# Two-layer hybrid attention and SwiGLU trunk on one core: the fifth pair of the down projection joins the two-step Strassen scheme, and the top steps move forward

## The chip, the cores and the metric

The kernel runs on one core of a Trainium2 chip. A core has five engines with queues of their own: TensorE (PE, matmuls), VectorE (DVE), ScalarE (ACT), GpSimd (POOL) and SyncE (SP, here the queue of the DMAs). The metric is the device time of one execution in microseconds (us); a lower one is better.

## What is computed

Two layers over a sequence of 256 tokens of width 1024, all in fp32. The part that the change touches is the last statement of each layer, the SwiGLU block and its down projection (`D_FF` is 2816):

```python
def hybrid_layer(x, ...):
    h = rms_norm(x, g_attn_pre)
    proj = einsum(h, w_in) + b_in
    ...                                  # MoBA and sliding-window attention
    x = x + rms_norm(einsum(mix, w_out), g_attn_post)
    h = rms_norm(x, g_ffn_pre)
    f = silu(h @ w_gate) * (h @ w_up)
    x = x + rms_norm(f @ w_down, g_ffn_post)
```

## The kernel before

**Tiling.** The tokens are two tiles `t` of 128. Weights come from HBM in blocks of 128 x 2048 numbers (1 MB) in the order of the list `BLOCKS`, each into one of three places of `raw`. ScalarE writes a rounded copy of a block (`hi`, L698) into one of four slots `w_h`, VectorE writes what the rounding left (`lo`, L985) into `w_l`, and TensorE multiplies block b as high x high, high x low and low x high, three matmuls for each product. A block of four k-tiles and 512 columns, or of two k-tiles and 1024 columns, costs 24 matmuls for both token tiles. `hi` of block b waits until TensorE is through with block b - 4 (`after(L, b)` handles block b + 4), and a load waits for the `lo` of the block that had its place.

**The SwiGLU part.** `FF` is cut into six chunks `c` of 512 columns (the last has 256). A chunk from 1 to 4 has four blocks, gate twice and up twice; chunk 5 has two. When both are multiplied, VectorE forms f (`swiglu`, L1189) and transposes it in blocks of 32 (`squares_f`, L1200), and GpSimd carries the 32-blocks across partitions with 16 copies (`exchange`, L638). ScalarE and VectorE then split the result into high and low parts in chunk c + 1 (`hi_f`, `lo_f` L1207).

**The down projection** is f (two token tiles, 22 k-tiles) times `w_down` (two halves of 512 columns). For k-tile pairs 0 to 4 the 2 x 2 x 2 block product is done by Strassen's scheme in Winograd's form with seven products in place of eight. Four of them (M1, M6, M5, M7) are summed over the pairs in banks 4 to 7 and are joined once at the end (`join`, L1258); three go straight into the result banks. The sums of f that the scheme needs, s1 to s4, are made by VectorE for the pairs of chunks 0, 1 and 2 (`add_s` L1217 to L1220, then `hi_s` on ScalarE L745 and `lo_s` on VectorE L1225). The sums of the weights are made in `raw` by `add_top` (L1235 to L1239, five instructions of 512 columns), which waits for the block's load.

- Pairs 0 to 3 go in two steps. The **top** step (`top(L, n)`, 12 matmuls, L1514) does the four shared products. It stands behind the last block of chunk n + 2, and waits for the low part of its block, of f, and of the sums s of chunk n // 2 (`summed`). The **bottom** step (`bottom(L, n)`, 9 matmuls) does the other three, between the down blocks, with half a block loaded again and the kept sum T4.
- Pair 4 goes in one piece, `squares`, behind the last bottom step: its block is loaded raw, VectorE makes all sums (`add_squares`, L1248 to L1252), and there are two splits of it, "raw" (1536 columns) and "sum" (2048 columns, `lo` at L976), for 9 and 12 matmuls.

The rest of the k-tiles (10 to 21) are plain down blocks: two among the bottom steps, four behind them ("late" ones, from `FIRST_LATE` on). The first late block is multiplied by token tile 0 only after `join_first` has added to its banks.

**What sets the order.** Each engine's program is written out by hand and runs strictly in order; they meet by counting semaphores. In chunk 1 VectorE's program ends with swiglu, the two transposes, `lo` of the next block, and then `lo_s(L, 0)`; the first `add_top` opens its part of chunk 2.

## Time and profile before

| | us |
|---|---|
| median of 3 runs | 562.53 |
| lowest, highest | 562.33, 562.94 |
| the profiled execution | 562.32 |
| its span | 560.5 |
| TensorE busy | 552.5 |
| VectorE busy | 454.7 |
| ScalarE busy | 308.7 |
| GpSimd busy | 248.9 |

The profiled execution's time is 1.8 us above its span, and 0.2 us under the median. The busy time of TensorE counts a matmul until its modelled end, which overlaps the next one's start: what one matmul costs is the distance between two starts in the timeline, and a short pause shows there as a longer distance, often without being listed as a wait.

### The profile page before, as it was taken

What the parts mean: (1) busy time and instruction counts of PE and PEld (TensorE: products, weight loads), DVE (VectorE), ACT (ScalarE), POOL (GpSimd) and SP (SyncE); (2) the same over time, 40 slices, a digit from 0 to 9 for tenths busy, and PEclk for the clock granted to TensorE, in tenths of its full rate; (3) what the DMA queues carried; (4) which work ended last, traced back from release to release, by engine and by line L of the source; (5) the groups of instructions that cost most, each with busy time, mean ns of one, the idle gap of its engine ahead of it and who ended that gap; (6) DMA issues with size and microseconds to landing.
All of it is one profiled execution on the core that took longest, in us unless ns stands there. A gap on an engine that the chain in (4) does not pass through costs nothing.

```text
span 560.5 us, 8816 instructions
## 1 busy us (share of the span) xinstructions
PE 552.5 (99%) x3346; PEld 454.1 (81%) x3346; DVE 454.7 (81%) x592; ACT 308.7 (55%) x438; POOL 248.9 (44%) x307
## 2 busy tenths in 40 slices
PE   8999999999999999999999999999999999999996
PEld 6878888888888888887888888888888888888774
DVE  6799996856879788789898998675848889878993
ACT  6576775555444633566547658574643635436540
POOL 1101132406396786954220055232076696965910
PEclk9999999999999999999999999999999999999999
DMA  8964533648445654477566344425573546536821
GB/s 347 373 227 145 202 105 161 229 160 313 163 177 220 232 195 187 146 255 269 227 248 214 134 170 151 187 88 215 229 258 151 224 151 230 209 124 197 291 76 75
DMA packets 19195, 111.55 MB, mean 199 GB/s; under 512 B 2384, under 2 KB 2768, under 8 KB 7632
## 3 DMA queue, kind: packets, MB, share of 16 engines
q1 hardware_dynamic: 19152, 110.97, 53.7%
q8 instruction: 27, 0.44, 0.3%
q14 instruction: 16, 0.13, 0.1%
HBM read 109.92 MB, written 1.05 MB: 198 GB/s over the span
## 4 chain that ended last, share of the span: by engine, by line
PE 47%; POOL 22%; DVE 16%; issue 5%; ACT 5%; DMA 4%; DVEq 0%; SPq 0%; POOLq 0%; ACTq 0%
PE bank L1499 39%; POOL work L638 20%; DVE w_l L985 4%; DMA raw<-in_w_blocks 3%; PE bank L1612 3%; DVE work L1200 2%; POOL mixed_crossed L622 2%; ACT w_h L698 2%; PE bank L1597 2%; PE bank L1638 1%; DMA work<-in_first_rest 1%; PE bank L1514 1%; DVE work L1189 1%; DVE fT_l L1207 1%; PE bank L1665 1%
## 5 line engine op out<-in xcount | busy, mean ns | idle before, releaser
L985 DVE TENSOR_TENSOR w_l<-raw,w_h 128x2048 fp32r<-128x2048 f32 x90 | 206.6, 2307 | 58.4 <-ACT w_h L698 58.0
L638 POOL COPY work<-work 32x256 f32<-32x256 f32 (+1 forms) x192 | 188.6, 982 | 107.4 <-DVE work L1200 79.8
L698 ACT ACTIVATE w_h<-raw 128x2048 fp32r<-128x2048 f32 x90 | 169.7, 1904 | 109.1 <-DVE raw L1239 65.5
L1499 PE MATMUL bank<-w_h,actT_h 128*128 128x512 f32 (+1 forms) x568 | 223.6, 394 | 0.2
L1499 PE MATMUL bank<-w_h,actT_l 128*128 128x512 f32 (+1 forms) x568 | 219.9, 387 | 0.0
L1499 PE MATMUL bank<-w_l,actT_h 128*128 128x512 f32 (+1 forms) x568 | 218.0, 386 | 0.0
L1499 PEld LDWEIGHTS bank<-w_h,actT_h 128*128 128x128 f32 x568 | 106.8, 188 | 23.1 <-issue 2.0
L1499 PEld LDWEIGHTS bank<-w_h,actT_l 128*128 128x128 f32 x568 | 106.7, 188 | 22.0
L1499 PEld LDWEIGHTS bank<-w_l,actT_h 128*128 128x128 f32 x568 | 106.8, 188 | 20.3
L612 POOL TENSOR_TENSOR norms<-norms,constants 128x1 f32<-128x1 f32 x8 | 4.8, 601 | 93.8 <-ACT bank L814 93.6
L787 ACT ACTIVATE work<-bank,neg_max 128x128 f32<-128x128 f32 (+1 forms) x64 | 25.9, 425 | 9.9 <-DVE neg_max L1102 9.9
L1612 PE MATMUL bank<-ident,work 128*128 128x128 f32 x216 | 29.6, 273 | 0.0
L1612 PEld LDWEIGHTS bank<-ident,work 128*128 128x128 f32 x216 | 25.4, 140 | 4.3
L1514 PE MATMUL bank<-w_h,fT_h 128*128 128x512 f32 x70 | 27.5, 393 | 0.3 <-DVE w_l L976 0.2
L1514 PE MATMUL bank<-w_l,fT_h 128*128 128x512 f32 x70 | 27.3, 390 | 0.0
L1514 PE MATMUL bank<-w_h,fT_l 128*128 128x512 f32 x70 | 27.2, 389 | 0.0
L587 POOL TENSOR_TENSOR norms<-norms,constants 128x1 f32<-128x1 f32 x8 | 10.8, 1354 | 36.9 <-ACT work L755 36.9
L622 POOL COPY mixed_crossed<-mixed_squares 32x128 f32<-32x128 f32 x48 | 19.2, 399 | 13.7 <-DVE mixed_squares L1139 11.8
L764 ACT ACTIVATE work<-bank 128x512 f32<-128x512 f32 x16 | 9.6, 599 | 28.4 <-PE bank L1499 28.4
L595 POOL TENSOR_TENSOR norms<-norms,constants 128x1 f32<-128x1 f32 x8 | 6.6, 822 | 40.2 <-ACT work L764 40.2
L1154 DVE TENSOR_TENSOR work<-bank,gain_b 128x512 f32<-128x512 f32 x16 | 10.7, 687 | 12.6 <-ACT work L764 12.6
L1499 PE MATMUL bank<-w_h,fX_h 128*128 128x512 f32 x64 | 20.6, 393 | 0.2
(123 smaller groups left out, 635.2 us busy)
## 6 DMA issues: line engine op xcount, KB each, us to landing
raw<-in_w_blocks SPq DMA_DIRECT2D x90, 1024.0 KB, 4.8
raw<-in_w_blocks SPq DMA_DIRECT2D x8, 512.0 KB, 4.2
gains<-in_b_in SPq DMA_DIRECT2D x8, 256.0 KB, 5.7
work<-in_first_rest SPq DMA_DIRECT2D x3, 512.0 KB, 6.1
raw<-in_second_block SPq DMA_DIRECT2D x2, 512.0 KB, 8.1
x<-in_x SPq DMA_DIRECT2D x2, 512.0 KB, 13.8
gain_b<-in_g_attn_post SPq DMA_DIRECT2D x2, 512.0 KB, 8.1
gains<-in_g_ffn_pre SPq DMA_DIRECT2D x2, 512.0 KB, 6.9
```

The source lines that it names most:

```text
L587: nc.gpsimd.tensor_tensor(ss_x[:, t:t + 1], ss_x[:, t:t + 1], eps, ALU.add).then_inc(eps_added, 1)
L622: ins = nc.gpsimd.tensor_copy(mixed_crossed[t][32 * j:32 * j + 32, i * P:(i + 1) * P], mixed_squares[t][32 * i:32 * i + 32, j * P:(j + 1) ...
L638: ins = nc.gpsimd.tensor_copy(work[32 * j:32 * j + 32, 4:6, i * n:(i + 1) * n], work[32 * i:32 * i + 32, 6:8, j * n:(j + 1) * n])
L698: nc.scalar.activation(w["h"][:, slot(L, b), at:], raw[:, r, at:], ACT.Copy).then_inc(hi_ready, 1)
L787: last = nc.scalar.activation(probs[g, r][:, j, n * keys:(n + 1) * keys], bank[b][:, n * keys:(n + 1) * keys], ACT.Exp, bias=neg_max[:, g, ...
L985: nc.vector.tensor_tensor(w["l"][:, slot(L, b), at:], raw[:, raw_slot(L, b), at:], w["h"][:, slot(L, b), at:].bitcast(F32), ALU.subtract). ...
L1154: nc.vector.tensor_tensor(y[t][:, c, :], bank[b][:], gain_b[:, c * BANK:(c + 1) * BANK], ALU.mult).then_inc(drained[b], 1)
L1200: nc.vector.transpose(squares[t][:, 0:n].rearrange("p (j k b) -> p j k b", j=4, b=32), f[t][:, 0:n].rearrange("p (k j b) -> p j k b", j=4, ...
L1499: ins = nc.tensor.matmul(bank[BANK_OF[name]][:, 0:n], left[s][:, k, :], right[r][:, k, c * BANK:c * BANK + n], start=first and k == 0 and ...
L1514: ins = nc.tensor.matmul(out_[:], left[s], right[r], start=first and (s, r) == ("h", "h"), stop=last and (s, r) == ("l", "h"))
L1597: ins = nc.tensor.matmul(bank[BANK_OF[name]][:, 0:n], actT[s][:, k, tokens(t)], right[r][:, k, :], start=first, stop=last and (s, r) == pr ...
L1612: ins = nc.tensor.transpose(out_[:, q * P:(q + 1) * P], src(q), ident[:])
```

## The change

- **Pair 4 goes in two steps** like the others: `TOPS` is 5, `squares`, `add_squares`, the blocks "raw" and "sum" and their splits are gone. There is a fifth top block, `top(L, 4)` behind the last block of chunk 5, a fifth bottom block, and a tile `t4_last` for its T4. The matmuls are the same in number: 12 + 9 for the pair in either form.
- **The top steps move forward.** `top(L, n)` for n from 0 to 3 stands behind the first block of chunk n + 2, ahead of the chunk's other blocks. In VectorE's program `add_top(L, n)` moves from the chunk of its use into the chunk ahead of it, `add_top(L, 0)` into chunk 1.
- **Loads.** The half blocks of bottom steps 0 and 1 come in one load of 1 MB, as do those of 2 and 3; the fifth is loaded alone.
- **Joining.** M1 is copied out (`keep_m1`) already behind the last top step, and the two sums that only need the top products are made earlier (`sum_products`).

The diff, its core:

```diff
 CHUNK_AT = []
-TOPS = 4
+TOPS = 5
 TOP_AT = []
 for c in range(FFN_CHUNKS):
     CHUNK_AT += [len(BLOCKS)]
     if c < FF // BANK:
-        BLOCKS += [(m, k, 4, c * BANK, BANK) for m in ("gate", "up") for k in (0, 4)]
+        parts = [(m, k, 4, c * BANK, BANK) for m in ("gate", "up") for k in (0, 4)]
     else:
-        BLOCKS += [("both", k, 4, c * BANK, BANK) for k in (0, 4)]
+        parts = [("both", k, 4, c * BANK, BANK) for k in (0, 4)]
+    BLOCKS += parts[:1]
     if c >= 2:
         TOP_AT += [len(BLOCKS)]
         BLOCKS += [("top", 2 * (c - 2), 2, 0, D)]
+    BLOCKS += parts[1:]
 LAST = FFN_CHUNKS - 1
-LAST_COLS = FF - LAST * BANK
+TOP_AT += [len(BLOCKS)]
+BLOCKS += [("top", 2 * TOPS - 2, 2, 0, D)]
+
+
+def part_at(c, q):
+    return CHUNK_AT[c] + q + (1 if c >= 2 and q else 0)
+
+
 FIRST_DOWN = len(BLOCKS)
 KF = FF // P
 
 
 
 
...
         BLOCKS += [("bot", 2 * len(BOT_AT) - 2, 2, 0, D)]
-RAW_AT = len(BLOCKS)
-BLOCKS += [("raw", 2 * TOPS, 2, 0, D), ("sum", 2 * TOPS, 2, 0, D)]
+BOT_AT += [len(BLOCKS)]
+BLOCKS += [("bot", 2 * TOPS - 2, 2, 0, D)]
 FIRST_LATE = len(BLOCKS)
 BLOCKS += [("down", k, 2, 0, D) for k in (14, 16, 18, 20)]
 NB = len(BLOCKS)
-LOADED = [b for b in range(NB) if BLOCKS[b][0] != "sum"]
+
+LOADED = [b for b in range(NB) if b not in BOT_AT[1::2]]
 NL = len(LOADED)
 STORED = [b for b in LOADED if BLOCKS[b][0] != "bot"]
...
+    return L * NL + LOADED.index(b - 1 if b in BOT_AT[1::2] else b)
 
 
 def raw_slot(L, b):
@@ -118,6 +127,11 @@
     return (load_count(L, b) // RAW + 1) * 16
 
 
+def bot_cols(b):
+    at = BOT_AT.index(b) % 2
+    return slice(2 * BANK * at, 2 * BANK * (at + 1))
+
+
 def freed_by(b):
...
                     past_L, past = divmod(load_count(L, b) - RAW, NL)
-                    place_free(lo_ready, past_L * NB + LOADED[past] + 1)
-                    if BLOCKS[LOADED[past]][0] == "raw":
-                        place_free(sums_ready, past_L + 1)
+                    place_free(lo_ready, past_L * NB + LOADED[past] + (2 if LOADED[past] in BOT_AT[:-1] else 1))
                 if BLOCKS[b][0] == "bot":
-                    top = STORED.index(TOP_AT[BOT_AT.index(b)])
-                    sp.dma_start(raw[:, r, 0:2 * BANK], w_blocks[L, top, :, 2 * BANK:4 * BANK]).then_inc(raw_in[r], 16)
+                    n = BOT_AT.index(b)
+                    at = [STORED.index(top) for top in TOP_AT[n:n + 2]]
+                    tops = slice(at[0], at[-1] + 1, at[-1] - at[0] or 1)
+                    sp.dma_start(raw[:, r, 0:2 * BANK * len(at)].rearrange("p (a n) -> p a n", a=len(at)),
+                                 w_blocks[L, tops, :, 2 * BANK:4 * BANK].rearrange("a p n -> p a n")
+                                 ).then_inc(raw_in[r], 16)
                 else:
...
 
-                act.wait_ge(block_used, USED.done(L, FIRST_LATE - 2) + USED.n)
+                act.wait_ge(block_used, USED.done(L, TOP_AT[-1]) + USED.n)
                 nc.scalar.activation(m1_sum, products[0][:], ACT.Copy).then_inc(m1_kept, 1)
...
                 for c in range(1, FFN_CHUNKS):
-                    b = CHUNK_AT[c]
-                    after(L, b)
+                    after(L, part_at(c, 0))
+                    if c >= 2:
+                        after(L, TOP_AT[c - 2])
                     silus(L, c, 0)
                     silus(L, c, 1)
-                    after(L, b + 1)
+                    after(L, part_at(c, 1))
                     if c < FFN_CHUNKS - 1:
-                        after(L, b + 2)
+                        after(L, part_at(c, 2))
                         hi_f(L, c - 1, 0)
                         hi_f(L, c - 1, 1)
                         if c <= FAST_CHUNKS:
                             hi_s(L, c - 1)
-                        after(L, b + 3)
-                    if c >= 2:
-                        after(L, TOP_AT[c - 2])
+                        after(L, part_at(c, 3))
+                    else:
+                        after(L, TOP_AT[TOPS - 1])
                 hi_f(L, FFN_CHUNKS - 2, 0)
                 hi_f(L, FFN_CHUNKS - 2, 1)
-                for b in range(FIRST_DOWN, RAW_AT):
+                after(L, FIRST_DOWN)
...
+                keep_m1(L)
+                for b in range(FIRST_DOWN + 1, FIRST_LATE - 2):
                     after(L, b)
-                keep_m1(L)
                 hi_f(L, FFN_CHUNKS - 1, 0)
                 hi_f(L, FFN_CHUNKS - 1, 1)
-                after(L, RAW_AT)
-                after(L, RAW_AT + 1)
+                after(L, FIRST_LATE - 2)
+                after(L, FIRST_LATE - 1)
                 sum_y(L, 1, 0)
                 if L < depth - 1:
...
                 x = bank[BANK_OF["down", t, c]]
                 nc.vector.tensor_tensor(x[:], x[:], what, ALU.add).then_inc(joined, 1)
 
-            def join_first(L):
+            def sum_products(L):
 
                 _, m6, m5, _ = products
                 dve.wait_ge(m1_kept, L + 1)
+                link(L, nc.vector.tensor_tensor(u2, m1_sum, m6[:], ALU.add))
+                link(L, nc.vector.tensor_tensor(u4, u2, m5[:], ALU.subtract))
+
+            def join_first(L):
+
+                dve.wait_ge(products_full, L + 1)
                 join(L, 0, 0, m1_sum)
-                dve.wait_ge(products_full, 3 * L + 1)
-                link(L, nc.vector.tensor_tensor(u2, m1_sum, m6[:], ALU.add))
-                dve.wait_ge(products_full, 3 * L + 2)
-                link(L, nc.vector.tensor_tensor(u4, u2, m5[:], ALU.subtract))
                 join(L, 0, 1, u4)
 
             def join_second(L):
 
                 _, _, m5, m7 = products
-                dve.wait_ge(products_full, 3 * L + 3)
                 link(L, nc.vector.tensor_tensor(u3, u2, m7[:], ALU.add))
                 dve.wait_ge(second_begun, L + 1)
                 join(L, 1, 0, u3)
...
                 for c in range(1, FFN_CHUNKS):
-                    b = CHUNK_AT[c]
-                    end = b + (1 if c == FFN_CHUNKS - 1 else 3)
-                    if 2 <= c < FFN_CHUNKS - 1:
-                        add_top(L, c - 2)
-                    if c == FFN_CHUNKS - 1:
-                        swiglu(L, c, 0)
-                    for q in range(b, end):
-                        after(L, q)
+                    after(L, part_at(c, 0))
+                    if c >= 2:
+                        after(L, TOP_AT[c - 2])
                     if c < FFN_CHUNKS - 1:
+                        add_top(L, c - 1)
+                        after(L, part_at(c, 1))
+                        after(L, part_at(c, 2))
                         if c <= FAST_CHUNKS:
                             add_s(L, c - 1)
                         lo_f(L, c - 1, 0)
@@ -1398,30 +1389,29 @@
                         squares_f(L, c, 1)
                         if c == FFN_CHUNKS - 2:
                             add_top(L, TOPS - 1)
-                        after(L, end)
+                        after(L, part_at(c, 3))
                         if c <= FAST_CHUNKS:
                             lo_s(L, c - 1)
                     else:
+                        swiglu(L, c, 0)
+                        after(L, part_at(c, 1))
                         swiglu(L, c, 1)
-                        after(L, end)
-                    if c >= 2:
-                        after(L, TOP_AT[c - 2])
+                        after(L, TOP_AT[TOPS - 1])
                 for t in range(T):
                     lo_f(L, FFN_CHUNKS - 2, t)
                 for t in range(T):
                     squares_f(L, FFN_CHUNKS - 1, t)
                 after(L, FIRST_DOWN)
                 after(L, BOT_AT[0])
-                add_squares(L)
+                sum_products(L)
                 after(L, BOT_AT[1])
                 after(L, BOT_AT[1] + 1)
                 after(L, BOT_AT[2])
                 join_first(L)
                 after(L, BOT_AT[3])
-                after(L, RAW_AT)
                 lo_f(L, FFN_CHUNKS - 1, 0)
                 lo_f(L, FFN_CHUNKS - 1, 1)
-                after(L, RAW_AT + 1)
+                after(L, BOT_AT[4])
                 join_second(L)
                 scale_y(L, 1, 0)
                 update_x(L, 1, 0)
...
                 pe.wait_ge(lo_ready, L * NB + b + 1)
-                product(m1, a11, b11, n == 0, False)
-                product(m6, s2, t2, n == 0, False)
-                product(m5, s1, t1, n == 0, False)
-                product(m7, s3, t3, n == 0, False).then_inc(block_used, 1)
+                last = n == TOPS - 1
+                product(m1, a11, b11, n == 0, last)
+                product(m6, s2, t2, n == 0, last)
+                product(m5, s1, t1, n == 0, last)
+                product(m7, s3, t3, n == 0, last).then_inc(block_used, 1)
                 USED.tick(b)
 
             def bottom(L, n):
...
-                product(x12, s4, b22, False, False)
-                product(x11, a12, b21, False, False)
-                product(x21, a22, t4, False, False).then_inc(block_used, 1)
+                last = n == TOPS - 1
+                product(x12, s4, b22, False, last)
+                ins = product(x11, a12, b21, False, last)
+                if last:
+                    ins.then_inc(products_full, 1)
+                product(x21, a22, t4, False, last).then_inc(block_used, 1)
                 USED.tick(b)
-
-            def squares(L):
-
...
                 multiply(L, 1, b + 2)
                 multiply(L, 1, b + 3)
                 for c in range(1, FFN_CHUNKS):
-                    b = CHUNK_AT[c]
                     for q in range(2 if c == FFN_CHUNKS - 1 else 4):
-                        multiply(L, 0, b + q)
-                        multiply(L, 1, b + q)
-                    if c >= 2:
-                        top(L, c - 2)
+                        multiply(L, 0, part_at(c, q))
+                        multiply(L, 1, part_at(c, q))
+                        if c >= 2 and q == 0:
+                            top(L, c - 2)
+                top(L, TOPS - 1)
...
```

**VectorE, chunk 1 of layer 0, before.** The rows are, in turn, swiglu twice, the two transposes, `lo` of a block, `lo_s(0)` (L1225), and then the first `add_top` (five rows).

```order
L1189 SCALAR_TENSOR_TENSOR work<-bank3,norms,work 128x512 [waits squares_ready0,drained2,full3]
L1189 SCALAR_TENSOR_TENSOR work<-bank1,norms,work 128x512 [waits squares_ready1,drained0,full1]
L1200 STREAM_TRANSPOSE work<-work 128x512 [waits crossed_in,drained3]
L1200 STREAM_TRANSPOSE work<-work 128x512 [waits crossed_in,drained1]
L985 TENSOR_TENSOR w_l<-raw,w_h 128x2048 [waits hi_ready]
L1225 TENSOR_TENSOR fT_l<-work,fT_h 128x1024 [waits s_hi_ready]
L1235 TENSOR_TENSOR raw<-raw 128x512 [waits raw_in1]
L1236 TENSOR_TENSOR raw<-raw 128x512
L1237 TENSOR_TENSOR gains<-raw 128x512
L1238 TENSOR_TENSOR gains<-gains,raw 128x512 [waits dve_step]
L1239 TENSOR_TENSOR raw<-raw 128x512
```

**VectorE, the same place now** (its lines are numbered 6 higher in the changed file): `add_top(0)` is the rows L1241 to L1245, then `lo` of two blocks, then `add_s(0)`.

```order
L1241 TENSOR_TENSOR raw<-raw 128x512 [waits raw_in1]
L1242 TENSOR_TENSOR raw<-raw 128x512
L1243 TENSOR_TENSOR gains<-raw 128x512
L1244 TENSOR_TENSOR gains<-gains,raw 128x512 [waits dve_step]
L1245 TENSOR_TENSOR raw<-raw 128x512
L991 TENSOR_TENSOR w_l<-raw,w_h 128x2048 [waits hi_ready] x2
L1223 TENSOR_TENSOR work<-work 128x256 [waits crossed_in]
L1224 TENSOR_TENSOR work<-work 128x256
L1225 TENSOR_TENSOR work<-work 128x256 [waits dve_step]
```

The rest of the chunk, down to `lo_s(0)` (L1231):

```order
L1195 SCALAR_TENSOR_TENSOR work<-bank3,norms,work 128x512 [waits squares_ready0,drained2,full3]
L1195 SCALAR_TENSOR_TENSOR work<-bank1,norms,work 128x512 [waits squares_ready1,drained0,full1]
L1206 STREAM_TRANSPOSE work<-work 128x512 [waits crossed_in,drained3]
L1206 STREAM_TRANSPOSE work<-work 128x512 [waits crossed_in,drained1]
L991 TENSOR_TENSOR w_l<-raw,w_h 128x2048 [waits hi_ready]
L1231 TENSOR_TENSOR fT_l<-work,fT_h 128x1024 [waits s_hi_ready]
L991 TENSOR_TENSOR w_l<-raw,w_h 128x2048 [waits hi_ready] x2
```

`lo_s(0)` keeps its place behind both swiglu and a `lo`, and the five additions have gone ahead of two `lo`.

**TensorE, chunk 2 of layer 0, behind its first block, before.** The next block follows.

```order
L1499 MATMUL bank0<-w_h,actT_h 128x512
L1499 MATMUL bank0<-w_l,actT_h 128x512
L1499 MATMUL bank0<-w_h,actT_l 128x512
L1499 MATMUL bank2<-w_h,actT_h 128x512 [waits lo_ready]
L1499 MATMUL bank2<-w_l,actT_h 128x512
L1499 MATMUL bank2<-w_h,actT_l 128x512
L1499 MATMUL bank2<-w_h,actT_h 128x512
```

**TensorE, the same place now.** L1504 with banks 4 to 7 is the top step.

```order
L1489 MATMUL bank0<-w_h,actT_h 128x512
L1489 MATMUL bank0<-w_l,actT_h 128x512
L1489 MATMUL bank0<-w_h,actT_l 128x512
L1504 MATMUL bank4<-w_h,fT_h 128x512 [waits lo_ready,s_lo_ready,f_lo_ready]
L1504 MATMUL bank4<-w_l,fT_h 128x512
L1504 MATMUL bank4<-w_h,fT_l 128x512
L1504 MATMUL bank5<-w_h,fT_h 128x512
```

The first top step now stands where the second block of chunk 2 stood; before, it came 72 matmuls (three blocks) later.

**VectorE, the end of layer 0, before:** `add_squares`, `lo` of "raw", of "sum" and of the first late block, `join_first`, two more `lo`.

```order
L981 TENSOR_TENSOR w_l<-gains,w_h 128x512
L979 TENSOR_TENSOR w_l<-raw,w_h 128x1024 [waits hi_ready]
L981 TENSOR_TENSOR w_l<-gains,w_h 128x512
L1248 TENSOR_TENSOR work<-raw 128x1024 [waits raw_in0]
L1251 TENSOR_TENSOR work<-work,raw 128x512 [waits dve_step]
L1252 TENSOR_TENSOR work<-raw,work 128x512 [waits dve_step]
L985 TENSOR_TENSOR w_l<-raw,w_h 128x1536 [waits hi_ready]
L976 TENSOR_TENSOR w_l<-work,w_h 128x2048 [waits hi_ready]
L985 TENSOR_TENSOR w_l<-raw,w_h 128x2048 [waits hi_ready]
L1258 TENSOR_TENSOR bank2<-bank2,work 128x512 [waits m1_kept]
L1266 TENSOR_TENSOR work<-work,bank5 128x512 [waits products_full]
```

**VectorE, the same place now:** `sum_products`, `lo` of the fifth bottom block, of two late blocks, `join_first`.

```order
L988 TENSOR_TENSOR w_l<-gains,w_h 128x512
L986 TENSOR_TENSOR w_l<-raw,w_h 128x1024 [waits hi_ready]
L988 TENSOR_TENSOR w_l<-gains,w_h 128x512
L1256 TENSOR_TENSOR work<-work,bank5 128x512 [waits m1_kept]
L1257 TENSOR_TENSOR work<-work,bank6 128x512 [waits dve_step]
L986 TENSOR_TENSOR w_l<-raw,w_h 128x1024 [waits hi_ready,dve_step]
L988 TENSOR_TENSOR w_l<-t4_last,w_h 128x512
L991 TENSOR_TENSOR w_l<-raw,w_h 128x2048 [waits hi_ready] x2
```

Three additions and two splits are gone; `join_first` has two instructions in place of four, and stands behind two late blocks in place of one.

## Rows read from the trace of the kernel before

**Rows 1.** the page, busy time of each engine: us, share of the span, instructions.
```profile
PE 552.5 (99%) x3346; PEld 454.1 (81%) x3346; DVE 454.7 (81%) x592; ACT 308.7 (55%) x438; POOL 248.9 (44%) x307
```

**Rows 2.** timeline of TensorE (start us, us, what), first matmuls of three top steps.
```profile
168.37 0.39 PE L1514 MATMUL bank<-w_h,fT_h 128*128 128x512 f32 x1
...
230.93 0.39 PE L1514 MATMUL bank<-w_h,fT_h 128*128 128x512 f32 x1
...
443.07 0.39 PE L1514 MATMUL bank<-w_h,fT_h 128*128 128x512 f32 x1
```

**Rows 3.** timeline of TensorE, end of layer 0.
```profile
254.50 0.39 PE L1514 MATMUL bank<-w_h,fT_l 128*128 128x512 f32 x1
254.95 0.50 PE L1514 MATMUL bank<-w_h,fT_h 128*128 128x512 f32 x1
...
257.85 0.39 PE L1499 MATMUL bank<-w_h,fX_h 128*128 128x512 f32 x1
...
261.70 0.39 PE L1499 MATMUL bank<-w_h,fX_l 128*128 128x512 f32 x1
...
262.71 0.62 PE L1499 MATMUL bank<-w_l,fX_h 128*128 128x512 f32 x2
```

**Rows 4.** timeline of TensorE, end of layer 1.
```profile
529.22 0.39 PE L1514 MATMUL bank<-w_h,fT_l 128*128 128x512 f32 x1
...
532.66 0.62 PE L1499 MATMUL bank<-w_h,fX_h 128*128 128x512 f32 x2
...
536.51 0.39 PE L1499 MATMUL bank<-w_h,fX_l 128*128 128x512 f32 x1
...
537.57 0.62 PE L1499 MATMUL bank<-w_l,fX_h 128*128 128x512 f32 x2
```

**Rows 5.** timeline of VectorE, end of layer 0.
```profile
227.95 4.69 DVE L985 TENSOR_TENSOR w_l<-raw,w_h 128x2048 fp32r<-128x2048 f32 x2 [1.99 <-ACT w_h L698]
...
252.50 2.40 DVE L976 TENSOR_TENSOR w_l<-work,w_h 128x2048 fp32r<-128x2048 f32 x1 [0.23 <-ACT w_h L690]
254.82 2.37 DVE L985 TENSOR_TENSOR w_l<-raw,w_h 128x2048 fp32r<-128x2048 f32 x1
...
259.75 4.48 DVE L985 TENSOR_TENSOR w_l<-raw,w_h 128x2048 fp32r<-128x2048 f32 x2
```

**Rows 6.** timeline of VectorE, chunk 1 of layer 0 and the step behind it.
```profile
132.50 2.48 DVE L985 TENSOR_TENSOR w_l<-raw,w_h 128x2048 fp32r<-128x2048 f32 x1 [1.49 <-ACT w_h L698]
...
143.38 2.29 DVE L985 TENSOR_TENSOR w_l<-raw,w_h 128x2048 fp32r<-128x2048 f32 x1 [2.52 <-ACT w_h L698]
...
148.11 1.40 DVE L1189 SCALAR_TENSOR_TENSOR work<-bank,norms,work 128x512 f32<-128x512 f32 x2
...
152.82 1.42 DVE L1225 TENSOR_TENSOR fT_l<-work,fT_h 128x1024 fp32r<-128x1024 f32 x1
154.16 0.88 DVE L1235 TENSOR_TENSOR raw<-raw 128x512 f32<-128x512 f32 x1
```

**Rows 7.** timeline of VectorE, layer 1.
```profile
427.52 1.42 DVE L1225 TENSOR_TENSOR fT_l<-work,fT_h 128x1024 fp32r<-128x1024 f32 x1
```

**Rows 8.** timeline of ScalarE, chunks 1 and 2 of layer 0.
```profile
141.43 1.92 ACT L698 ACTIVATE w_h<-raw 128x2048 fp32r<-128x2048 f32 x1 [3.01 <-PE bank L1499]
...
158.28 1.92 ACT L698 ACTIVATE w_h<-raw 128x2048 fp32r<-128x2048 f32 x1 [8.12 <-DVE raw L1239]
```

**Rows 9.** timeline of GpSimd, the exchange of chunk 0 (16 copies).
```profile
131.14 10.86 POOL L638 COPY work<-work 32x256 f32<-32x256 f32 x16 [20.02 <-DVE work L1200]
```

**Rows 10.** groups by line, GpSimd, from 131.1, 138.5 and 150.8 us on.
```profile
L638 POOL COPY work<-work 32x256 f32<-32x256 f32 x3 | 1.2, 393 | 20.1 <-DVE work L1200 20.0
...
L638 POOL COPY work<-work 32x256 f32<-32x256 f32 x2 | 2.8, 1379 | 0.1
...
L638 POOL COPY work<-work 32x256 f32<-32x256 f32 x7 | 7.4, 1059 | 9.1 <-DVE work L1200 8.8
```

**Rows 11.** a stretch behind the last matmul; the clock stands behind POOL.
```profile
555.00:559.00 4.00, 0.00 (x0) 0.00 (x0) 2.24 (x5) 0.69 (x2) 0.55 (x1) 0.93 0.20 73
```

More of the change, by code:

```diff
@@ L130, in completes @@
     m, k0, nk, col, n = BLOCKS[b]
-    if m in ("down", "raw", "sum", "top", "bot"):
+    if m in ("down", "top", "bot"):
         return [("down", t, c) for c in range(2)] if k0 + nk == KF else []
@@ L256, in trunk @@
         fT = {s: sb("fT_" + s, [P, 39, P], F32R) for s in "hl"}
-        sums = work_row[:, 0:4 * BANK].rearrange("p (a n) -> p a n", a=2)
-        t4_kept = [gains[:, n * BANK:(n + 1) * BANK] for n in range(TOPS)]
+        t4_kept = [gains[:, n * BANK:(n + 1) * BANK] for n in range(4)] + [sb("t4_last", [P, BANK])[:]]
         m1_sum = rope_tmp
@@ L672, in hi @@
                 m, k0 = BLOCKS[b][0:2]
-                if m == "sum":
-                    act.wait_ge(sums_ready, L + 1)
-                elif m == "top":
+                if m == "top":
                     r = raw_slot(L, b)
@@ L688, in hi @@
                     act.wait_ge(block_used, USED.done(L, last % NB) + (USED.n if last >= 0 else 0))
[L689 to L693 removed]
+                if m == "bot":
+                    nc.scalar.activation(w["h"][:, slot(L, b), 0:2 * BANK], raw[:, r, bot_cols(b)], ACT.Copy)
                     nc.scalar.activation(w["h"][:, slot(L, b), 2 * BANK:3 * BANK], t4_kept[BOT_AT.index(b)], ACT.Copy
@@ L973, in lo @@
                 m, k0 = BLOCKS[b][0:2]
-                if m == "sum":
-                    low, high = (w[s][:, slot(L, b), :].rearrange("p (a n) -> p a n", a=2) for s in "lh")
-                    nc.vector.tensor_tensor(low, sums, high.bitcast(F32), ALU.subtract).then_inc(lo_ready, 1)
-                elif m == "bot":
+                if m == "bot":
                     high, low = (w[s][:, slot(L, b), :] for s in "hl")
-                    nc.vector.tensor_tensor(low[:, 0:2 * BANK], raw[:, raw_slot(L, b), 0:2 * BANK],
+                    nc.vector.tensor_tensor(low[:, 0:2 * BANK], raw[:, raw_slot(L, b), bot_cols(b)],
                                             high[:, 0:2 * BANK].bitcast(F32), ALU.subtract)
@@ L1880 @@
     arrays["w_blocks"] = np.empty((depth, len(STORED), P, BLOCK), np.float32)
-    weights["raw"] = weights["down"].reshape(depth, FF, 2, BANK)[:, :, ::-1].reshape(depth, FF, D)
-    weights["top"] = weights["raw"]
+    weights["top"] = weights["down"].reshape(depth, FF, 2, BANK)[:, :, ::-1].reshape(depth, FF, D)
     for b, at in enumerate(STORED):
```

51 lines of the change are left out of this document (5 added, 46 removed).

## The prediction

> **What bounds the kernel now.** I read the page's busy times first: TensorE works 552.5 of 560.5 us [rows 1]. VectorE has a fifth of its time free, but runs in order, so its place in its program matters, not its sum. The change takes no matmul away (12 + 9 for pair 4 in either form), so the time can only move by TensorE's pauses. The list of waits hardly shows them; I looked for them in the timeline, as starts further apart than the pitch. The pitch: from the first matmul of the first top step to that of the fourth, at 168.37 and 230.93 [rows 2], lie three top steps and ten blocks, 3 x 12 + 10 x 24 = 276 matmuls, so 62.56 / 276 = 0.2267 us each.
>
> Between 254.50 and 257.85 [rows 3] stand 13 matmuls: 3.35 us where 2.95 would do, a pause of 0.40. It is the "sum" half of pair 4: its low part (L976) ends at 252.50 + 2.40 = 254.90 [rows 5], and the next matmul starts at 254.95. Of the 0.40, 0.22 are the wait and 0.18 the slow start behind it. Between 261.70 and 262.71 stand three matmuls (a row with "x2" between them): 1.01 for 0.68, a pause of 0.33; it waits for the `lo` of the second late block, which begins at 259.75 and takes 2.24 [rows 5]. Layer 1 has the same two, 3.44 - 2.95 = 0.49 and 1.06 - 0.68 = 0.38 [rows 4]. In all 1.60 us: that is everything the end of the layers can give back.
>
> **The change part by part.**
>
> *The first top step moves forward.* It was reached at 168.37 and comes three blocks, 72 x 0.2267 = 16.32 us, earlier: TensorE reaches it at 152.05. It waits for `lo_s(0)`, the low part of the sums s of chunk 0. VectorE does that at the end of its part of chunk 1: it starts at 152.82 and takes 1.42, so it is done at 154.24 [rows 6]. Before, that was 14 us of cover; now it is 2.2 us too late. With the lag of 0.05 seen at 254.90 / 254.95, TensorE starts again at 154.29: 2.24 us of waiting, and 0.15 for the slow start (0.18 above, here between that and 0.1). Nothing can run meanwhile, since TensorE's program is in order. Layer 1: 443.07 - 16.32 = 426.75 [rows 2] against 427.52 + 1.42 + 0.05 = 428.99 [rows 7], again 2.24. Cost: 2 x 2.39 = 4.8 us. The other three moved steps need the sums of chunks 0 and 1, made a chunk or more before, and wait for none.
>
> *`add_top(0)` in chunk 1 of VectorE.* Its five additions take from 154.16 [rows 6] until ScalarE starts at 158.28 [rows 8]: 4.1 us. They now stand behind the `lo` that ends at 134.98, and end at about 139.0; the block's `hi` takes 1.92, so its `lo` runs from 141.0 to 143.2. The next `lo`, at 143.38, waits for a `hi` of 141.43 that TensorE releases, and is not moved. VectorE idled here; its cover is 0.2 us, and everything behind 143.38, `lo_s(0)` too, stays where it was. So this costs nothing, if the exchange of chunk 0 is not held up. That one took 10.86 us from 131.14 to 142.0 [rows 9]; `add_s` needs it at 145.6 (the `lo` of 143.38 and 2.2). A copy takes 0.39 us beside an idle VectorE, 1.38 beside a `lo`, and 1.06 in a stretch with one `lo`, the `lo_s` and five additions, seven copies for seven instructions [rows 10]. I count 3 copies up to 132.5, 2 beside the `lo`, 5 beside the additions, 5 in the idle 2.0 us behind them, and the last beside the next `lo`: it ends by 143.2. I take 0. With 1.38 beside the additions too (3 copies), and 0.6 in the idle time, the last copy ends at 146.0 to 146.4: up to 0.8 us per layer, the upper end.
> The Trainium skill (SBUF — State Buffer, "Who interferes with whom") says that a VectorE instruction with two SBUF inputs and a GpSimd one that reads SBUF fully block each other for an instruction's length; by that rule copies pass between instructions and the five short additions let five through, which is the 0; by a rate in proportion to busy time it would be the 0.8 above. The seven for seven agree with the rule, the two beside one `lo` don't quite.
>
> *The other moved and added steps.* From chunk 2 on VectorE has as many steps per chunk as before. `add_top(4)` stands where `add_top(3)` stood. The low part of that block was done at 227.95 + 2.35 = 230.3 [rows 5], for a step reached at 230.93; top 4 is reached 12 matmuls later, a cover of 3.3 us. The pause above gives the helpers 2.2 us more on top. No cost, and if that cover were gone, TensorE would wait for the rest, one to one.
>
> *The end of the layer.* VectorE loses three additions and two splits (L976 alone 2.40) and gains one split of 1536 columns. The low part of the fifth bottom block comes before that of the first late block, long before use, so both old pauses go: -1.60 us. One new meeting is close. The first late block's `hi` waits for the down block ahead of bottom steps 2, 3, 4. Call that block's end T. ScalarE starts 0.26 behind such an end (141.43 against 152.05 - 48 x 0.2267 = 141.17), VectorE 1.95 later (143.38), two `lo` follow at 2.24 to 2.37 each [rows 5], then the join, a quarter of what `join_first` took, (259.75 - 257.19) / 4 = 0.64: T + 7.3 to 7.6. TensorE is there after 3 x 9 + 6 = 33 matmuls, T + 7.48. Between nothing and 0.25 with its slow start, I take 0.05 per layer: +0.1.
>
> *Loads.* One load of 1 MB more and four half ones turned into two whole and a half: SP's queue holds fewer, and no pause of TensorE stands behind a load. Price 0; a pair load comes from two places, whose speed no row shows, but it is asked for 8 us and more before its `hi`, against 5 for a load.
>
> **Sum:** 4.78 + 0.10 - 1.60 = +3.3 us. The profiled execution took 562.32, so 565.6; the median is 0.2 above it, so **565.7**.
>
> **The rivals.**
>
> *The exchange is held up.* Then `lo_s(0)` is 0.4 to 0.8 later in both layers, or the close meeting at the join costs 0.25 too: 565.7 + 1.6 = 567.3, at most 567.9. For it: GpSimd's copies are slow beside `lo`. Against: one copy per short instruction.
>
> *The clock falls in the pause.* In the 4 us from 555.0 on, with no matmul, the mean clock is 0.93 [rows 11]: full for 3.44 us, then the lower level, 1.2 for 2.4 GHz. The pause here is 2.2 us, with matmuls before and behind. If it fell all the same, matmuls would start 0.45 apart for a time; at 4 us of that per layer, 2 us each: 569.7.
> The Trainium skill (TensorE: Matmul & The Clock Gate, "HAM oscillation — how this bites in real kernels") tells of kernels whose clock falls in each wait between bursts of matmuls; that rule is this rival.
>
> *Not slower.* `lo_s(0)` would have to be done much earlier. VectorE has swiglu, transposes, a `lo` and `lo_s` behind the last matmul of chunk 1; these run from 148.11 to 154.24, 6.1 us [rows 6], while that matmul is done at 152.05 - 5.44 + 0.2 = 146.8. If the 1.3 us of backlog before them were gone, the pause would be 0.94 and the total 2 x (0.94 + 0.15) + 0.1 - 1.60 = +0.7, 563.2. It decides from 1.3 us of pause per layer down. Against: the diff leaves that backlog as it is, and sets more work before it. A gain of 1.1 would need a pause under 0.2, less than the 6.1 us of work allow after one block of 5.44.
>
> **How the numbers follow.** The forecast has 0.72, held up 0.16, the clock 0.05, not slower 0.04, and 0.03 for something else. The forecast alone spans 564.9 (a join without wait and slow starts of 0.05) to 566.6 (one layer held up, or the join at 0.25); with the first rival 567.9. The range 564.6 to 567.9 leaves out the clock and the not-slower case. A measurement tells 0.2%, 1.1 us, from no change: slower 0.94, same 0.04, faster 0.02.
>
> **What would show it.** In the changed kernel's timeline TensorE's first matmul into bank 4 of the first top step starts 2.2 us behind its predecessor's pitch, released by VectorE's low part of the sums (L1231), at about 154.3 and 428 to 429; `add_top(0)` ends near 139.0 and the exchange by 143 to 144; the pauses before the late blocks are gone. It is wrong if that matmul starts at 152, if `lo_s(0)` ends later than 155, or if the clock falls below full.

## The result: 1.0% slower, and out of the range

| | median us | runs us | ratio, 95% interval |
|---|---|---|---|
| before, beside it | 562.74 | 562.33 to 564.50 (6) | |
| changed | 569.45 | 566.61 to 569.68 (5) | 1.0103 (1.0078 to 1.0127) |
| forecast | 565.7 | 564.6 to 567.9 | |

Slower was right, the size was not: the medians lie 6.7 us apart, and 3.3 were forecast. (The ratio in the table is not that of the medians, 1.012, which lies inside its interval. Two executions of all that follow, 1434.51 us of the changed kernel and 695.71 us of the one with 4 matmuls in the pause, were disturbed, by what is not known, and are left out.) The profiled execution took 569.68 us, with a span of 567.9, 7.4 more than that of before.

The place that the prediction spoke of is the first top step of each layer. TensorE's timeline of the changed kernel, layer 0 (start us, us, what, idle time before and who ended it):

```profile
152.10 0.39 PE L1489 MATMUL bank<-w_h,actT_l 128*128 128x512 f32 x1
155.02 0.47 PE L1504 MATMUL bank<-w_h,fT_h 128*128 128x512 f32 x1 [2.53 <-issue]
155.32 0.40 PE L1504 MATMUL bank<-w_l,fT_h 128*128 128x512 f32 x1
...
156.49 0.59 PE L1504 MATMUL bank<-w_h,fT_h 128*128 128x512 f32 x1
156.88 0.63 PE L1504 MATMUL bank<-w_l,fT_h 128*128 128x512 f32 x1
157.31 0.63 PE L1504 MATMUL bank<-w_h,fT_l 128*128 128x512 f32 x1
...
160.13 0.39 PE L1489 MATMUL bank<-w_h,actT_h 128*128 128x512 f32 x1
```

The last matmul of the block starts at 152.10, the first of `top(L, 0)` at 155.02. Less the pitch that is a pause of 2.92 - 0.23 = 2.69 us; predicted were 2.24. The profile names no releaser ("issue"); VectorE's timeline below shows what it waits for. What follows it was hardly expected: matmuls start 0.24 apart for 1.5 us, and then 0.39 to 0.43 apart up to 159.87. From 155.02 to 160.13 stand 15 matmuls, 5.11 us where 3.40 would do: 1.71 us more. The windows give the reason (length; busy time and instructions of PE, PEld, DVE, ACT, POOL; the granted clock; DMA):

```profile
153.00:154.00 1.00, 0.00 (x0) 0.00 (x0) 1.00 (x2) 1.00 (x1) 0.96 (x2) 1.00 0.00 0
155.00:156.00 1.00, 0.98 (x4) 0.85 (x5) 1.00 (x1) 0.00 (x0) 0.96 (x2) 1.00 0.81 279
156.00:157.00 1.00, 1.00 (x5) 0.79 (x4) 1.00 (x1) 0.00 (x0) 1.00 (x1) 0.75 0.95 401
157.00:158.00 1.00, 1.00 (x4) 0.80 (x3) 0.32 (x1) 0.00 (x0) 0.96 (x2) 0.50 0.71 295
...
160.00:161.00 1.00, 1.00 (x6) 0.83 (x5) 0.00 (x0) 1.00 (x1) 0.92 (x3) 1.00 0.95 401
432.00:433.00 1.00, 0.00 (x0) 0.00 (x0) 1.00 (x2) 0.95 (x1) 0.96 (x2) 0.99 0.00 0
433.00:434.00 1.00, 0.54 (x1) 0.50 (x2) 1.00 (x2) 0.00 (x0) 0.96 (x2) 0.50 0.54 115
```

The granted clock is 1.00 all through the pause and for the first microsecond of work behind it, and falls in the next one to 0.50, the lower of its two levels (1.2 for 2.4 GHz), with TensorE busy. From 159.9 on it is full again. In layer 1 the same pause, and the clock is down when TensorE starts again:

```profile
430.55 0.39 PE L1489 MATMUL bank<-w_h,actT_l 128*128 128x512 f32 x1
433.46 0.77 PE L1504 MATMUL bank<-w_h,fT_h 128*128 128x512 f32 x1 [2.52 <-issue]
434.03 0.63 PE L1504 MATMUL bank<-w_l,fT_h 128*128 128x512 f32 x1
```

433.46 - 430.55 - 0.23 = 2.68 us of pause, and 8 matmuls in 3.28 us up to 436.74 where 1.81 would do: 1.47 more.

VectorE's timeline shows why the pause is longer than forecast:

```profile
135.16 0.88 DVE L1241 TENSOR_TENSOR raw<-raw 128x512 f32<-128x512 f32 x1
...
138.37 0.88 DVE L1245 TENSOR_TENSOR raw<-raw 128x512 f32<-128x512 f32 x1
141.23 4.73 DVE L991 TENSOR_TENSOR w_l<-raw,w_h 128x2048 fp32r<-128x2048 f32 x2 [1.98 <-ACT w_h L706]
146.26 0.43 DVE L1223 TENSOR_TENSOR work<-work 128x256 f32<-128x256 f32 x1 [0.30 <-POOL work L652]
...
148.79 1.40 DVE L1195 SCALAR_TENSOR_TENSOR work<-bank,norms,work 128x512 f32<-128x512 f32 x2
...
153.50 1.42 DVE L1231 TENSOR_TENSOR fT_l<-work,fT_h 128x1024 fp32r<-128x1024 f32 x1
```

`add_top(0)` (L1241 to L1245) ends at 139.2 and the two `lo` behind it end at 145.96, both as predicted (all starts in this trace are 0.28 later than before, from the start of the program on). But `add_s` (L1223) waits 0.30 us more, for GpSimd's exchange, and `lo_s(0)` (L1231) ends at 154.92, 0.40 behind 154.24 + 0.28. TensorE's first matmul of the top step starts 0.10 behind that end. The exchange itself took 14.82 us, against 10.86 [rows 9]. GpSimd's timeline, and its groups (mean ns last) beside one of the five additions, and beside the two `lo`:

```profile
131.40 14.82 POOL L652 COPY work<-work 32x256 f32<-32x256 f32 x16 [20.00 <-DVE work L1206]
...
L652 POOL COPY work<-work 32x256 f32<-32x256 f32 x2 | 1.5, 761 | 0.1
...
L652 POOL COPY work<-work 32x256 f32<-32x256 f32 x2 | 4.9, 2447 | 0.1
```

At the end of the layer the two pauses of [rows 3] are gone. TensorE goes over from the last bottom step to the late block at its pitch, and the join (L1250) is through in time. TensorE, then VectorE:

```profile
261.93 0.39 PE L1504 MATMUL bank<-w_h,fT_l 128*128 128x512 f32 x1
262.15 0.62 PE L1489 MATMUL bank<-w_h,fX_h 128*128 128x512 f32 x2
...
258.24 4.49 DVE L991 TENSOR_TENSOR w_l<-raw,w_h 128x2048 fp32r<-128x2048 f32 x2 [2.62 <-ACT w_h L706]
262.65 1.29 DVE L1250 TENSOR_TENSOR bank<-bank,work 128x512 f32<-128x512 f32 x2
```

**The balance** of the two profiled executions, both layers: pauses 2.69 + 2.68, the slow matmuls behind them 1.71 + 1.47, the start of the program 0.28, the old pauses -1.60. That is 7.2 of 7.4 us; the 0.2 left were not followed further.

### The profile page after: what moved, and what is told of

Its sections match the earlier page's. It is cut to its first block, busy times and chain, and to the rows that moved or that the text cites. A ratio compares the mean times of both kernels' runs of the same rounds, so it can differ in the third digit from the quotient of the medians.

```text
span 567.9 us, 8818 instructions
## 1 busy us (share of the span) xinstructions
PE 555.2 (98%) x3346; PEld 456.7 (80%) x3346; DVE 457.8 (81%) x598; ACT 312.8 (55%) x440; POOL 233.7 (41%) x307
## 4 chain that ended last, share of the span: by engine, by line
PE 87%; DVE 5%; POOL 3%; issue 2%; ACT 1%; DMA 1%; SPq 0%; DVEq 0%; POOLq 0%
PE bank L1489 71%; PE bank L1504 9%; PE bank L1585 3%; DVE w_l L991 3%; POOL mixed_crossed L636 2%; PE bank L1570 2%; PE bank L1611 1%; DMA work<-in_first_rest 1%; PE bank L1638 1%; ACT work L795 1%; DVE work L1138 1%; POOL norms L626 1%; POOL norms L627 0%; DVE mixed_squares L1145 0%; DVE work L1082 0%
## 5 line engine op out<-in xcount | busy, mean ns | idle before, releaser
L706 ACT ACTIVATE w_h<-raw 128x2048 fp32r<-128x2048 f32 x90 | 171.8, 1917 | 106.0 <-PE bank L1489 43.4
L652 POOL COPY work<-work 32x256 f32<-32x256 f32 (+1 forms) x192 | 174.2, 907 | 116.2 <-DVE work L1206 88.8
L1504 PE MATMUL bank<-w_h,fT_h 128*128 128x512 f32 x70 | 28.5, 407 | 5.1 <-issue 5.1
L835 ACT ACTIVATE work<-bank,norms 128x512 f32<-128x512 f32 (+1 forms) x24 | 15.6, 652 | 25.9 <-PE bank L1489 25.9
L1504 PE MATMUL bank<-w_h,fT_l 128*128 128x512 f32 x70 | 28.2, 403 | 0.0
L1504 PE MATMUL bank<-w_l,fT_h 128*128 128x512 f32 x70 | 28.2, 403 | 0.0
```

The costliest lines, as they stand in the source:

```text
L652: ins = nc.gpsimd.tensor_copy(work[32 * j:32 * j + 32, 4:6, i * n:(i + 1) * n], work[32 * i:32 * i + 32, 6:8, j * n:(j + 1) * n])
L706: nc.scalar.activation(w["h"][:, slot(L, b), :], raw[:, r, :], ACT.Copy).then_inc(hi_ready, 1)
L835: nc.scalar.activation(silu[t][:, 0:n], bank[b][:, 0:n], ACT.Silu, scale=rstd_x[:, t:t + 1]).then_inc(drained[b] if c < LAST else last_sil ...
L1504: ins = nc.tensor.matmul(out_[:], left[s], right[r], start=first and (s, r) == ("h", "h"), stop=last and (s, r) == ("l", "h"))
```

## The experiments

The questions: is the wait for `lo_s(0)` the whole cost, or does something else come late behind it? And is it the standing still that brings the clock down? Ratios are against the kernel before, timed on the same chip (its medians: 563.20 us beside `lo_s(0)` moved ahead and beside the 12 and the 4 matmuls, 562.83 beside the last experiment, 562.95 beside all others).

### `lo_s(0)` ahead of swiglu

```diff
                         lo_f(L, c - 1, 1)
+                        if c == 1:
+                            lo_s(L, 0)
                         swiglu(L, c, 0)
...
-                        if c <= FAST_CHUNKS:
+                        if 1 < c <= FAST_CHUNKS:
                             lo_s(L, c - 1)
```

> The changed kernel with one instruction moved per layer: VectorE does lo_s(0), the low part of the sums s of chunk 0, ahead of the two swiglu of chunk 1 in place of behind them and a lo. Theory A (the whole loss is TensorE's pause at the first top step, which waits for lo_s(0), and the fall of its clock that follows): lo_s(0) is done by about 150.5 us, TensorE comes to the step at 152.3, no pause, the clock stays full (0.998), and only the gain at the layers' ends is left: 562.6 - 1.6 = 561.0, up to 561.5. Rival B (the new order of the blocks or the additions in chunk 1 cost as such): a pause or a slower pitch stays somewhere, 565 or more.

Measured: 564.33 us (563.75 to 566.23, 11 runs), ratio 1.0025 (1.0015 to 1.0035). The pause at the first top step is gone as expected, and the clock stays full in the profiled execution, but the time is 3 us above the one expected. TensorE's timeline, at the first top step and at the first down block:

```profile
151.91 0.39 PE L1491 MATMUL bank<-w_h,actT_l 128*128 128x512 f32 x1
152.13 0.39 PE L1506 MATMUL bank<-w_h,fT_h 128*128 128x512 f32 x1
...
236.23 0.39 PE L1506 MATMUL bank<-w_h,fT_l 128*128 128x512 f32 x1
238.10 0.70 PE L1491 MATMUL bank<-w_h,fT_h 128*128 128x512 f32 x2 [1.49 <-DVE work L1195]
```

A new wait of 1.64 us stands at the first matmul of the down projection (1.74 in layer 1). It isn't for weights: it claims the banks out of which swiglu of chunk 5 (L1195) reads. VectorE's timeline:

```profile
235.24 1.41 DVE L986 TENSOR_TENSOR w_l<-raw,w_h 128x1024 fp32r<-128x1024 f32 x1
236.57 0.88 DVE L988 TENSOR_TENSOR w_l<-gains,w_h 128x512 fp32r<-128x512 f32 x1
237.37 0.47 DVE L1195 SCALAR_TENSOR_TENSOR work<-bank,norms,work 128x256 f32<-128x256 f32 x1
```

That swiglu stands in VectorE's program behind the split of the first bottom block (L986 and L988), and that one behind two `lo`, of top block 4 and of the first down block. The changed kernel has the same order; there TensorE came 2.7 us later, and the wait never showed: in an execution of it with a full clock (below) this swiglu ends at 238.14 and TensorE comes to the bank at 238.66. The pause hid a second fault.

### Matmuls to fill the pause

```diff
+                if n == 0:
+                    for _ in range(12):
+                        nc.tensor.matmul(bank[4][:], actT["h"][:, 4, 0:P],
+                                         actT["h"][:, 4:6, :].rearrange("p k n -> p (k n)"), start=True, stop=True)
                 summed(L, n)
```

The 12 matmuls go into bank 4, which the top step writes anew. The later two have 4 and 8 of them.

> The changed kernel with 12 matmuls of 512 columns more in front of the first top step of each layer, into a bank that the step then overwrites: 2.7 us of TensorE's work in the time in which it stood still. They take nothing away: the step still starts when lo_s(0) is done. Theory A (the clock falls because TensorE stands still): the clock stays full, span some 3.1 us under the changed kernel's 567.9, time 566.3 to 566.8. Rival C (the clock falls for another reason, as a state of the run or of the load): the clock still falls twice and the time is 569.5.

Measured: 566.44 us (566.37 to 566.56, 4 runs), ratio 1.0058 (1.0042 to 1.0073).

```profile
152.25 2.88 PE L1533 MATMUL bank<-actT_h 128*128 128x512 f32 x12
154.97 0.44 PE L1504 MATMUL bank<-w_h,fT_h 128*128 128x512 f32 x1
```

TensorE never stands still, `top(L, 0)` starts at the same time as in the changed kernel (154.97), and the clock stays full. The wait is all paid, 5.4 us in two layers, and the 3 us behind it are not.

> As the kernel with 12 matmuls more, but with 4: the first top step starts at the same time, and TensorE stands still for some 1.8 us in place of 2.7. If the clock follows the length of the standstill and 1.8 us don't suffice, 566.5 with the clock full; if any such pause will do, 569.5 with two falls; something between (one fall, 568) if it is a matter of where the pause lies.

Measured: 567.86, 566.47 and 566.62 us, ratio 1.0068 (1.0049 to 1.0086). The profiled execution was the one of 567.86, and there the clock fell in layer 1, behind 2.0 us without a matmul (431.42 - 429.18 for the fourth - 0.23), and again with matmuls at full pitch in between:

```profile
428.50 1.07 PE L1533 MATMUL bank<-actT_h 128*128 128x512 f32 x4
431.42 0.47 PE L1504 MATMUL bank<-w_h,fT_h 128*128 128x512 f32 x1 [1.86 <-issue]
...
432.52 0.63 PE L1504 MATMUL bank<-w_l,fT_h 128*128 128x512 f32 x1
432.94 0.63 PE L1504 MATMUL bank<-w_h,fT_l 128*128 128x512 f32 x1
```

With 8 matmuls and 0.9 us of standing still:

> As the kernel with 12 matmuls more, with 8: the first top step starts at the same time, TensorE stands still for 0.9 us. Nothing should bring the clock down: 566.5 in each execution. If some have 568, a pause this short will do as well, and the length of the standstill isn't what matters.

Measured: 566.56, 566.56, 567.04 and 567.14 us, ratio 1.0072 (1.0058 to 1.0085); none of them shows a step of 1.5 us.

### Without `add_top(0)`

The five additions are replaced by two of 8 columns. The weight sums of pair 0 are left out, so the top products of pair 0 are those of other numbers; all steps behind stay as many and as long.

```diff
+                if n == 0:
+                    link(L, nc.vector.tensor_tensor(t4[:, 0:8], b21[:, 0:8], b11[:, 0:8], ALU.subtract))
+                    nc.vector.tensor_tensor(t4[:, 8:16], b21[:, 8:16], b11[:, 8:16], ALU.subtract
+                                            ).then_inc(tops_ready, 1)
+                    return
```

> The changed kernel with the five additions of add_top(0) left out (two of 8 columns stand in their place, so the results of pair 0 are not the reference's). It asks what the additions in chunk 1 cost through the exchange of chunk 0. Theory D (they hold up GpSimd's copies, and so add_s and lo_s(0)): the exchange takes 11 to 12 us in place of 14.8, add_s(0) starts 0.3 to 0.4 earlier without waiting for it, and the pause at the first top step is 2.3 in place of 2.7. Rival E (they cost nothing): the pause stays at 2.7.

One execution took 565.86 us, at a mean granted clock of 0.999. TensorE's timeline, then GpSimd's:

```profile
152.10 0.39 PE L1494 MATMUL bank<-w_h,actT_l 128*128 128x512 f32 x1
154.62 0.47 PE L1509 MATMUL bank<-w_h,fT_h 128*128 128x512 f32 x1 [2.13 <-issue]
```

```profile
131.39 10.90 POOL L652 COPY work<-work 32x256 f32<-32x256 f32 x16 [19.99 <-DVE work L1206]
```

Without the additions the exchange takes 10.90 us, `add_s` waits for nothing, and the pause is 154.62 - 152.10 - 0.23 = 2.29 us, the 2.24 of the prediction and 0.05 more of lag (`lo_s(0)` ends at 154.52, so the lag is 0.10). So what `add_top(0)` costs by way of the exchange is 0.40 us per layer, and the rest of the 2.69 is `lo_s(0)`. Timed later on another chip:

> The kernel without the additions of add_top(0), in more executions (the results of pair 0 are not the reference's). Its two pauses are 2.3 us long. If a pause of that length doesn't bring the clock down, all executions have 565.9 and a clock of 0.997 or more, and the additions in chunk 1 cost 0.8 us by themselves and the rest through the clock; if the first look was chance, some have 567.4 or 568.9.

Measured: 565.74, 565.68, 565.83 and 567.58 us, ratio 1.0061 (1.0045 to 1.0076).

### The changed kernel again

> The changed kernel itself, on this chip, to count how often the clock falls: two pauses of 2.7 us per execution. From five executions so far seven falls in ten pauses: 569.5 with two, 568.2 with one, 566.6 with none.

Measured: 565.83, 569.39, 567.33 and 569.63 us, ratio 1.0107 (1.0086 to 1.0127). The profiled execution, that of 565.83, has the pauses (2.74 and 2.69) and no fall of the clock in either layer:

```profile
151.29 0.39 PE L1489 MATMUL bank<-w_h,actT_l 128*128 128x512 f32 x1
154.26 0.47 PE L1504 MATMUL bank<-w_h,fT_h 128*128 128x512 f32 x1 [2.58 <-issue]
154.57 0.39 PE L1504 MATMUL bank<-w_l,fT_h 128*128 128x512 f32 x1
```

Here is the price of the slow start alone: 0.31 for 0.23, 0.08 us.

The nine times of the changed kernel stand in three heaps: 565.83 and 566.61; 567.33 and 568.19; 569.39 to 569.68 (five). Their middles lie 1.5 to 1.8 us apart, and the traces have no fall in the lowest heap and two in the highest. The mean granted clock of each execution goes roughly the same way: 0.999 and 0.998 in the lowest heap, 0.996 and 0.995 in the middle one, 0.991 to 0.996 in the highest. Read so, with one fall for each heap upwards:

| kernel | us without a matmul | pauses | falls |
|---|---|---|---|
| changed | 2.7 | 18 | 12 |
| without `add_top(0)` | 2.3 | 10 | 1 |
| 4 matmuls in the pause | 1.8 to 2.0 | 6 | 1 |
| 8 matmuls | 0.9 | 8 | 0 |
| 12 matmuls | 0 | 8 | 0 |

Only three of these falls were seen in a trace (two in the first, one in the third row); the others are read from times. Four of the changed kernel's nine executions, four of the five without `add_top(0)` and all with 8 matmuls ran on one chip: there it is 5 falls in 8 pauses, 1 in 8 and 0 in 8. The 12 matmuls ran on another, for which no execution of the changed kernel is on record, and on which the 4 matmuls had their fall. The first experiment has one time of 11 (566.23) two us above its others, so a fall is likely there too, behind a wait of 1.7 us.

### One and two of chunk 5's swiglu moved forward too

The next step takes the first experiment and mends what it laid bare: swiglu of chunk 5 for token tile 0 goes ahead of the split of the first bottom block, right behind those of top block 4 and of the first down block.

```diff
                     after(L, part_at(c, 0))
+                    if c == FFN_CHUNKS - 1:
+                        swiglu(L, c, 0)
...
                     else:
-                        swiglu(L, c, 0)
                         after(L, part_at(c, 1))
                         swiglu(L, c, 1)
```

> The kernel with lo_s(0) moved ahead, and with one more instruction per layer moved: VectorE does the swiglu of chunk 5, token tile 0, right behind the low parts of top 4 and of the first down block, in place of behind those of the first bottom block too. Theory F (with the pause at the first top step gone, TensorE waits 1.64 and 1.74 us at the first down block for the bank that this swiglu drains, because the pause had given VectorE that time before): the swiglu ends at 235.7 against TensorE's 236.4, both waits go, and the time is 564.3 - 3.4 = 560.9, some 2 us or 0.4% under the kernel before on the same chip (563.2). Rival (VectorE is simply full, and the wait moves to the next block that it is late with): 562.5 or more, with a pause at the first bottom step.

Measured: 563.61 us (563.35 to 563.94, 11 runs), ratio 1.0011 (1.0002 to 1.0019). Missed again, and nearer to the rival: the wait moved on, not to the first bottom step but to the middle of the same down block, where token tile 1 begins, on the bank that the second swiglu reads (it starts at 239.92 on VectorE). It is 1.47 us in layer 0, by the distance of the starts:

```profile
238.53 0.61 PE L1492 MATMUL bank<-w_h,fT_l 128*128 128x512 f32 x2
240.45 0.74 PE L1492 MATMUL bank<-w_h,fT_h 128*128 128x512 f32 x2 [1.30 <-DVE work L1195]
```

So both have to move:

```diff
                     if c == FFN_CHUNKS - 1:
                         swiglu(L, c, 0)
+                        swiglu(L, c, 1)
...
                         after(L, part_at(c, 1))
-                        swiglu(L, c, 1)
```

> The kernel with lo_s(0) and the first swiglu of chunk 5 moved ahead, and the second swiglu of chunk 5 (token tile 1) too: VectorE does both right behind the low parts of top 4 and of the first down block, ahead of both bottom steps' splits. In the kernel without this TensorE waits 1.30 and 1.06 us, in the middle of the first down block, for bank 0, which the second swiglu drains at 240.4. Theory F (each of these waits is one instruction in the wrong place, and only the pause at the first top step had hidden them): it ends at 236.3, TensorE comes for the bank at 239.1, no wait, 563.6 - 2.4 = 561.2, some 0.3% under the kernel before (562.95 in the same company). Rival (VectorE is full): the splits of the bottom steps, 0.9 later now, become late for TensorE's 241.8, and the time stays at 562.5 or more.

Measured: 560.86 us (560.17 to 561.05, 5 runs), **ratio 0.9962 (0.9949 to 0.9976)**: faster than both kernels. VectorE's timeline, and the profile's whole list of TensorE's waits (us in total, times, longest):

```profile
235.69 0.86 DVE L1195 SCALAR_TENSOR_TENSOR work<-bank,norms,work 128x256 f32<-128x256 f32 x2
236.47 1.21 DVE L986 TENSOR_TENSOR w_l<-raw,w_h 128x1024 fp32r<-128x1024 f32 x1
```

```profile
PE bank L1582 <- DVE work L1274: 1.5, 1, 1.5
PE bank L1492 <- DVE actT_l L1020: 0.2, 1, 0.2
```

Both swiglu are through at 236.5; TensorE begins the down block at 236.42, 0.09 behind its pitch. No listed wait is left in the part that the change touches (that of 1.5 us is in the kernel before too), and the median is 1.97 us under that of before: the 1.60 us of the old pauses, and 0.4 that no trace was searched for. So VectorE was not full, it was in the wrong order.

## Why the prediction was right in direction and wrong in size

**The bound and where to look: right.** All but 0.5 of the 7.4 us are TensorE's pauses and its clock; no matmul was added or taken away.

**The first top step: right, 0.05 low.** The 2.24 us of waiting were read from [rows 2, 6]. Without the additions it measured 2.29; the lag was 0.10, not 0.05. The slow start was taken as 0.15 and measured 0.08.

**`add_top(0)` "costs nothing, if the exchange is not held up": wrong by 0.40 us per layer.** The additions did fit into VectorE's idle time, and left every `lo` in place. The exchange ended at 146.2, not by 143.2. The fault is in my reading of [rows 10]: "x2 | 2.8, 1379" is the mean of two unlike copies. Taken one by one, the copies of the kernel before are these (a window each from 138.5 and from 139.0), with the `lo` beside them:

```profile
138.45 2.40 DVE L985 TENSOR_TENSOR w_l<-raw,w_h 128x2048 fp32r<-128x2048 f32 x1 [3.48 <-ACT w_h L698]
...
L638 POOL COPY work<-work 32x256 f32<-32x256 f32 x1 | 0.4, 393 | 0.0
...
L638 POOL COPY work<-work 32x256 f32<-32x256 f32 x1 | 2.4, 2365 | 0.0
```

So one copy stands beside a `lo`, for the whole of its length, and not two of 1.38. In the changed kernel the 16 copies go 4 ahead of the `lo` of 132.78, 1 beside it (2.35 us), 5 beside the five additions (0.76 each), 4 in the idle time behind them, and 1 beside each of the two `lo` that now stand back to back (2.49 and 2.40). I had counted 3, 2, 5, 5 and 1. Two copies were left when the two `lo` began, and so the last one ended 0.26 us behind the second `lo`. The first rival held a delay of 0.4 to 0.8, with a chance of 0.16; its lower end came true, but by luck: it had 3 slow copies beside the additions, and there were 5 at 0.76.
The Trainium skill (SBUF — State Buffer, "Who interferes with whom") has a VectorE instruction with two SBUF inputs and a GpSimd one that reads SBUF lock each other out. The trace agrees, for one copy per `lo` and per addition, in both kernels. I had quoted the rule and then counted against it at the `lo`.

**The clock: the step that failed.** It was a rival at 0.05 and 2 us per layer, and in the sum it stood at nothing. Its price was near (3.0 us in both layers, priced at 4); the chance was wrong. I argued from [rows 11], where the clock stayed full for 3.44 us from 555.0 on with no matmul, against a fall in 2.2 us. That row is one execution of one place. In the changed kernel the clock was full through the 2.7 us and fell 1.5 us after TensorE had begun again, and in 12 of 18 pauses by the times. A full clock at the end of a pause says nothing of the clock behind it. The filled pauses show that the standing still brings it about: with 12 or 8 matmuls in it, and the top step begun at the same time, no fall is seen in 16 places (two executions by their traces, six by their times). And the two misses may work together: with the pause at the forecast's 2.3 us the fall came once in ten, by the counts, so the 0.4 us of the exchange seem to have brought most of the falls as well. That is read from counts, and that kernel differs in its five additions too; it is not shown.
The Trainium skill (TensorE: Matmul & The Clock Gate, "HAM oscillation — how this bites in real kernels") tells of a clock that falls in the waits between bursts of matmuls; its example has waits of some 3 to 5 us for a DMA. The trace agrees that it happens, and has it behind 2.69 us without a matmul; the rival deserved more than 0.05.

**The other moved steps: "no cost" was true for the wrong reason.** I gave top step 4 a cover of 3.3 us, and added that the pause gives the helpers time. I didn't follow the step that comes behind it in VectorE's program: swiglu of chunk 5, which frees the banks for the down blocks. With the pause its cover was 0.52 us; without the pause 1.64 and 1.74 us are missing. That made the price of the "not slower" rival wrong as well: it gave 563.2 for a shorter pause, and with no pause at all the kernel took 564.3.

**The end of the layer: right.** -1.60 us came, and the close meeting at the join cost nothing where I had put 0.05.

**The sum.** Pauses 5.4 (4.5), slow start 0.2 (0.3), join 0 (0.1), old pauses -1.6: +4.0 for +3.3, and with a full clock the changed kernel takes 565.8 to 566.6, inside the range. The clock's 3.0 us brought it out. Two slips in the working changed nothing of this: the median before and the sum, 562.53 + 3.28, give 565.8 and not 565.7, and a join without wait and slow starts of 0.05 take 0.3 off, which is 565.4 and not 564.9 for the low end.

## What to carry to other kernels

When a step is moved ahead of its helper, follow the helper engine's program past that step too: the next things it does are late by as much, and a pause may be what hides them. Price a pause of TensorE at its length and at what the clock may take behind it, and take a full clock in one pause as no bound for the next. GpSimd's copies beside VectorE's `tensor_tensor` went by instructions here: two long ones in a row let two copies through, however short these are alone. And before the mean of two instructions is used as a duration, take the two apart: 1.38 us was 0.39 and 2.37.
